# Two blocks on one core: high parts before low parts behind three norms, and the attention norm's scale inside its products

## What is computed

```
first block:
  h = rms_norm(x) * (1 + scale1) + shift1
  x = x + g1 * (hybrid mixer(h) @ w_o)
  h = rms_norm(x) * (1 + scale2) + shift2                 # norm N1 of the kernel
  x = x + g2 * ((silu(h @ w_fi[:, :F]) * (h @ w_fi[:, F:])) @ w_fo)
  x = rms_norm(x) * (1 + scale_f) + shift_f               # norm N2, the final modulate
second block:
  y = rms_norm(x, attn_norm)                              # norm N3
  q, k, v = split(y @ w_qkv);  x = x + attention(q, k, v) @ w_o2
  y = rms_norm(x, ffn_norm)                               # norm N4
  u = causal_conv(y @ w_up) + bias;  x = x + (silu(gate) * val) @ w_down
  out = rms_norm(x, final_norm)                           # norm N5
rms_norm(x, w) = x * rsqrt(mean(x * x) + eps) * w
```

## Time and profile before

| | |
|---|---|
| median of 3 runs | 975.1 us (972.58 to 975.62) |
| profiled execution, its own time | 974.01 us |
| its span in the profile | 972.2 us |
| PE busy | 926.5 us, 95% of the span, 7,996 matmuls |
| PE weight loads busy | 880.7 us, 91% |
| DVE busy | 667.2 us, 69% |
| ACT busy | 504.9 us, 52% |
| POOL busy | 65.2 us, 7% |
| mean granted clock of PE, as a share of full | 0.983 |

### The profile page before, as it was taken

One profiled execution on the slowest core, in us unless ns is written; L12 is line 12 of the kernel. 1 busy time (PEld: TensorE's weight loads), 2 busy tenths in 40 slices (PEclk: granted clock), 3 DMA queues, 4 the chain that ended last, 5 costly groups with the idle time before them and its releaser, 6 DMA issues.

```text
span 972.2 us, 18558 instructions
## 1 busy us (share of the span) xinstructions
PE 926.5 (95%) x7996; PEld 880.7 (91%) x7996; DVE 667.2 (69%) x1113; ACT 504.9 (52%) x821; POOL 65.2 (7%) x91
## 2 busy tenths in 40 slices
PE   5789999999999999999989999989999999999997
PEld 2588888898899999989989999979998999999997
DVE  3876677557579986778758875465656677777643
ACT  2476666544344556455334444465565566665442
POOL 0100012011000000030000001010000300000001
PEclk9799999999999999999999999999999999999999
DMA  8743222232249985446898775515343345555631
GB/s 321 265 157 127 88 88 91 85 131 88 88 158 359 351 299 219 174 179 253 253 290 318 265 241 186 197 43 197 131 140 108 107 177 196 186 174 166 235 120 44
DMA packets 27681, 177.31 MB, mean 182 GB/s; under 512 B 2864, under 2 KB 5680, under 8 KB 7504
## 3 DMA queue, kind: packets, MB, share of 16 engines
q1 hardware_dynamic: 27600, 176.13, 51.5%
HBM read 174.29 MB, written 1.84 MB: 181 GB/s over the span
## 4 chain that ended last, share of the span: by engine, by line
PE 71%; DVE 12%; ACT 7%; DMA 7%; issue 2%; SPq 0%; DVEq 0%; ACTq 0%
PE ps L1002 38%; PE ps L1008 19%; DVE wl L1696 3%; DMA raw<-in_w_fi_dram 3%; DVE acc L1631 2%; ACT wh L1343 2%; PE ps L1000 2%; DMA raw<-in_ada_dram 1%; DMA raw<-in_w_rest_dram 1%; DVE tmp L1658 1%; PE ps L1046 1%; DMA raw<-in_w_sc_dram 1%; PE ps L1140 1%; PE ps L1054 1%; PE ps L1201 1%
## 5 line engine op out<-in xcount | busy, mean ns | idle before, releaser
L1002 PE MATMUL ps<-HH,wh 128*128 128x256 f32 x1480 | 388.0, 294 | 6.4 <-DVE wl L1696 5.5
L1696 DVE TENSOR_TENSOR wl<-raw,wh 128x1024 fp32r<-128x1024 f32 x265 | 321.4, 1233 | 97.2 <-ACT wh L1343 96.5
L1002 PE MATMUL ps<-HH,wl 128*128 128x256 f32 x1480 | 375.2, 285 | 0.0
L1343 ACT ACTIVATE wh<-raw 128x1024 fp32r<-128x1024 f32 x265 | 272.6, 1040 | 171.8 <-PE ps L1008 105.3
L1002 PEld LDWEIGHTS ps<-HH,wh 128*128 128x128 f32 x1480 | 287.1, 194 | 15.8 <-issue 8.0
L1002 PEld LDWEIGHTS ps<-HH,wl 128*128 128x128 f32 x1480 | 287.1, 194 | 2.1 <-issue 2.1
L1008 PE MATMUL ps<-HL,wh 128*128 128x256 f32 x1480 | 241.5, 286 | 2.6 <-DVE HL L1671 2.2
L1008 PEld LDWEIGHTS ps<-HL,wh 128*128 128x128 f32 x1480 | 207.3, 194 | 3.3 <-DVE HL L1671 2.6
L1002 PE MATMUL ps<-FH,wl 128*128 128x256 f32 x352 | 88.8, 285 | 0.0
L1002 PE MATMUL ps<-FH,wh 128*128 128x256 f32 x352 | 88.1, 279 | 0.0
L1631 DVE SCALAR_TENSOR_TENSOR acc<-raw,silc,acc 128x512 f32<-128x512 f32 x101 | 76.6, 758 | 8.4 <-DMA raw<-in_ada_dram 5.2
(11 more groups left out here) (251 smaller groups left out, 1090.1 us busy)
## 6 DMA issues: line engine op xcount, KB each, us to landing
raw<-in_ada_dram SPq DMA_DIRECT2D x32, 1024.0 KB, 5.3
raw<-in_w_fi_dram SPq DMA_DIRECT2D x22, 1024.0 KB, 4.9
raw<-in_w_up_dram SPq DMA_DIRECT2D x22, 1024.0 KB, 4.8
raw<-in_w_rest_dram SPq DMA_DIRECT2D x20, 1024.0 KB, 4.8
raw<-in_w_in_dram SPq DMA_DIRECT2D x16, 1024.0 KB, 4.8
raw<-in_w_qkv_dram SPq DMA_DIRECT2D x12, 1024.0 KB, 4.8
raw<-in_w_o_dram SPq DMA_DIRECT2D x8, 1024.0 KB, 4.7
raw<-in_w_fo_dram SPq DMA_DIRECT2D x8, 1024.0 KB, 4.9
```

The lines of the kernel that those rows point to most:

```text
L1002: e.matmul(o, w[:, k, 128 * t:128 * t + 128], x_hi[:, k0 + k, :], start=first and n + k == 0, **MM)
L1343: e.activation(whl[u % HALF][0][:, 0:n], raw[i % RAW][:, c:c + n], ACT.Copy).then_inc(*a_hi.up(u))
L1696: e.tensor_tensor(wl[:, 0:n], raw[i % RAW][:, c:c + n], wh[:, 0:n].bitcast(F32), ALU.subtract).then_inc(*v_lo.up(u))
```

## The change

Five things:

1. Behind N1, N3 and N4 the low parts are no longer made between the scalings. `apply` writes all four `scale` and `high` events, then four `low` events; DVE makes all eight low parts, POOL none. The shift of N1 is one instruction per tile.
2. The two products behind each of these norms run through `high_first`: the 64 matmuls on the high activation of all four units, then the 32 on the low activation. The call of `split_up_to` in it goes no further than the fifth unit; the next units are put into the list only behind both products.
3. N2 and N3 share one R. `tmp = X * R` serves both: ACT makes `HH` from it with the weights `w1n` and `shn` (scale and shift times the attention norm's weight), DVE writes the block's output into X (`stream`) and the low part from X. The products `q2`, `k2`, `v2` then run on activations without N3's own scale.
4. N3's scale `R3` is made later: ACT squares the output, POOL adds the squares, and `third_scale` puts one summing matmul, Ln, Exp, and a copy times 0.125 (`R3q`) behind `k2` 0. `norm_col` turns R3 into a column for `v2`.
5. `q2` and `k2` are evacuated by DVE (`normed`, times R3q or R3) in place of ACT, `v2` by two ACT copies with the column as scale. The second sum of squares and its nine matmuls of no use are gone. `mod_scale` stands before `close`.

The function `in_turns` is added and called by nothing. The diff, cut:

```diff
-            if j:
-                parts(n, j - 1)
-        parts(n, 3)
+            emit("high", n, j, held[j])
+        for j in range(4):
+            if n == N3:
+                emit("stream", j, held[j])
+            emit("low", n, j, held[j])
+            tmp.give(held[j], v_norm, "lo", n, 2 * j + 1)
+            if n == N3:
+                s, before = sq.take()
+                emit("sq", N3, j, s, before, part[0] if j else None)
+                if j:
+                    sq.give(part[0], g_norm, "part", N3, j)
+                part[:] = [s]
...
+    def third_scale():
+        misc.order[:] = [b for b in misc.order if b[0] == 3]
+        bank, before = misc.take()
+        emit("norm_sum", N3, part[0], bank, before)
+        sq.give(part[0], p_norm, "sum", N3)
+        emit("norm_r", N3, bank)
+        made.add("norm_r3")
+        misc.give(bank, a_norm, "ln", N3)
+        yield
+        yield
+        bank, before = yield from take(misc)
+        emit("norm_col", N3, bank, before)
+        made.add("norm_col")
+        misc.give(bank, a_norm, "col")
+    def scaled_out(p):
+        kind, j, bank = p["kind"], p["j"], p["banks"][0]
+        while ("norm_col" if kind == "v2" else "norm_r3") not in made:
+            yield
+        if kind == "v2":
+            emit("plain", p["p"], 0)
+            main.give(bank, a_ev, "plain", p["p"])
+        else:
+            emit("normed", p["p"], 0)
+            main.give(bank, v_ev, "normed", p["p"])
+        made.add((kind, j))
+        if kind == "k2":
+            tasks.extend(attend(h) for h in range(4 * j, 4 * j + 4))
...
         elif kind in ("q2", "k2", "v2"):
-            emit("plain", p["p"], 0)
-            main.give(banks[0], a_ev, "plain", p["p"])
-            made.add((kind, j))
-            if kind == "k2":
-                tasks.extend(attend(h) for h in range(4 * j, 4 * j + 4))
+            begin(scaled_out(p))
...
-                bank, before = misc.take()
-                for i in range(4):
-                    emit("shift", n, i)
-                    if i:
-                        s, sfree = sq.take()
-                        emit("norm_sq", N3, i - 1, s, sfree, bank, before if i == 1 else None)
-                        sq.give(s, p_norm, "sq", N3, i - 1)
-                s, sfree = sq.take()
-                emit("norm_sq", N3, 3, s, sfree, bank, None)
-                sq.give(s, p_norm, "sq", N3, 3)
-                wbank, wfree = misc.take()
-                emit("norm_r", N3, bank, wbank, wfree)
-                misc.give(wbank, p_norm, "warm", N3)
-                misc.give(bank, a_norm, "ln", N3)
-                apply(N3)
-                misc.order[:] = [b for b in misc.order if b[0] == 3]
-            elif n == N4:
-                apply(n)
+            close(n, p)
+            for t in range(2):
+                main.give(banks[t], v_ev, "x", n, 6 + t)
+            if n == N5:
+                emit("finish")
             else:
-                emit("finish")
+                apply(N3 if n == N2 else n)
...
+    def open_banks(p):
+        count = 2 if p["split"] else 1
+        while len(main.order) < count:
+            assert tasks
+            tick()
+        taken = [main.take() for _ in range(count)]
+        p["banks"] = [b for b, _ in taken]
+        p["free"] = [f for _, f in taken]
+    def run_unit(p, n, last=None, part=None):
+        u = p["units"][n]
+        if part != "low":
+            split_up_to(u + HALF - 1 if last is None else last)
             low_of(u)
             if n == 0:
-                count = 2 if p["split"] else 1
-                while len(main.order) < count:
-                    assert tasks
-                    tick()
-                taken = [main.take() for _ in range(count)]
-                p["banks"] = [b for b, _ in taken]
-                p["free"] = [f for _, f in taken]
+                open_banks(p)
             until(*operands_of(p, units[u]))
-            tiles = p["width"] // 128
-            for t in range(tiles):
-                emit("mm", u, t)
-                if (n, t) != (len(p["units"]) - 1, tiles - 1):
-                    tick()
+        tiles = p["width"] // 128
+        for t in range(tiles):
+            emit("mm", u, t, part)
+            if part == "high" or (n, t) != (len(p["units"]) - 1, tiles - 1):
+                tick()
+    def close_product(p):
         after(p)
         tick()
...
+    def high_first(ps):
+        last = ps[0]["units"][0] + HALF - 1
+        for p in ps:
+            for n in range(2):
+                run_unit(p, n, last, "high")
+        for p in ps:
+            for n in range(2):
+                run_unit(p, n, last, "low")
+            close_product(p)
+    together = {("fg", 0): (high_first, ("fu", 0)), ("q2", 0): (high_first, ("k2", 0)),
+                ("ug", 0): (high_first, ("uv", 0))}
...
+        if key in together:
+            way, second = together[key]
+            way([p, named[second]])
+            if key == ("q2", 0):
+                begin(third_scale())
+        elif key not in [second for _, second in together.values()]:
+            for n in range(len(p["units"])):
+                run_unit(p, n)
+            close_product(p)
...
-    def pe_product(e, u, t):
+    def pe_product(e, u, t, part):
...
-        if first:
+        if first and part != "low":
             free(e, p["free"][b])
         v_lo.wait_ge(e, u)
-        for k in range(kn):
+        for k in range(kn) if part != "low" else ():
             high_of(e, src, k0 + k)
             for n, w in enumerate((wh, wl)):
...
-        for k in range(kn):
+        for k in range(kn) if part != "high" else ():
             low_part(e, src, k0 + k)
...
-        ins.then_inc(*p_mm.up(u, t))
+        if part != "high":
+            ins.then_inc(*p_mm.up(u, t))
...
-            a_ev.wait_ge(e, "plain", named["q2", j]["p"])
-            a_ev.wait_ge(e, "plain", named["k2", j]["p"])
+            v_ev.wait_ge(e, "normed", named["q2", j]["p"])
+            v_ev.wait_ge(e, "normed", named["k2", j]["p"])
...
+            elif kind == "norm_col":
+                b = ev[2]
+                free(e, ev[3])
+                a_norm.wait_ge(e, "r", N3)
+                for t in range(2):
+                    ins = e.matmul(psum[b][:, t:t + 1], R3[0:1, cs[t]], ones[0:1, 0:1], start=True, **MM)
+                ins.then_inc(*p_norm.up("col"))
+            elif kind == "norm_sum":
+                _, n, s, b, before = ev
+                free(e, before)
+                g_norm.wait_ge(e, "part", n, 3)
+                e.matmul(psum[b][:, 0:T], ones, sqs[s][:, 0:T], start=True, **MM).then_inc(*p_norm.up("sum", n))
...
+    def act_high(e, n, j, m):
+        finished(e, named[before_write[n]])
+        for kt in (2 * j, 2 * j + 1):
+            src, dst = tmps[m][:, T * (kt % 2):T * (kt % 2) + T], HH[:, kt, :]
+            v_norm.wait_ge(e, "scaled", n, kt)
+            if n == N1:
+                mod_ready(e, 6, 7)
+                ins = e.activation(dst, src, ACT.Identity, bias=modc[:, 24 + kt:25 + kt])
+            elif n == N3:
+                v_norm.wait_ge(e, "w1n")
+                ins = e.activation(dst, src, ACT.Identity, scale=w1n[:, kt:kt + 1], bias=shn[:, kt:kt + 1])
+            else:
+                ins = e.activation(dst, src, ACT.Copy)
+            ins.then_inc(*a_norm.up("hi", n, kt))
...
+        if n == N3 and j > 1:
+            x_ready(e, N2, 2 * j)
+            x_ready(e, N2, 2 * j + 1)
+            e.tensor_tensor(pair(tmps[m]), X[:, 2 * j:2 * j + 2, :], R[:, None, :].broadcast_to([128, 2, T]),
+                            ALU.mult).then_inc(*v_norm.up("scaled", n, 2 * j + 1))
+            v_norm.at[("scaled", n, 2 * j)] = v_norm.at[("scaled", n, 2 * j + 1)]
+            return
...
+    def dve_stream(e, j, m):
+        mod_ready(e, 12, 13)
+        v_norm.wait_ge(e, "w1c", N2, 0)
+        for kt in (2 * j, 2 * j + 1):
+            v_norm.wait_ge(e, "scaled", N3, kt)
+            e.tensor_scalar(X[:, kt, :], tmps[m][:, T * (kt % 2):T * (kt % 2) + T], w1c[:, kt:kt + 1],
+                            modc[:, 48 + kt:49 + kt], ALU.mult, ALU.add).then_inc(*v_norm.up("stream", kt))
+    def dve_low(e, n, j, m):
+        for kt in (2 * j, 2 * j + 1):
+            src, high = tmps[m][:, T * (kt % 2):T * (kt % 2) + T], HH[:, kt, :].bitcast(F32)
+            a_norm.wait_ge(e, "hi", n, kt)
+            if n == N1:
+                ins = e.scalar_tensor_tensor(out=HL[:, kt, :], in0=src, scalar=modc[:, 24 + kt:25 + kt], in1=high,
+                                             op0=ALU.add, op1=ALU.subtract)
+            elif n == N3:
+                v_norm.wait_ge(e, "stream", kt)
+                ins = e.scalar_tensor_tensor(out=HL[:, kt, :], in0=X[:, kt, :], scalar=v("attn_norm", kt), in1=high,
+                                             op0=ALU.mult, op1=ALU.subtract)
+            else:
+                ins = e.tensor_tensor(HL[:, kt, :], src, high, ALU.subtract)
...
```

(11 more changed lines are left out.)

137 lines of the change are left out of this document (63 added, 74 removed).

## The result

The changed kernel takes 982.23 us (median of four runs, 981.08 to 986.08), the kernel before 974.68 beside it: a ratio of 1.0103, with a 95% interval of 1.0071 to 1.0135. It is slower, by 1.0%. The profiled execution took 981.08 us, its span is 979.2; before it was 972.2.

What follows compares the result with a forecast made beforehand. PE was taken as the bound, busy 95% of the span, losing time only in waits or at half clock. Net losses of 2.1 + 2.4 + 4.1 = 8.6 us on 974.0 gave 982.6, forecast as 983 us, range 976 to 989.

Steps and rivals of the forecast that it cites:

- Entries: Losses at the norms shrink: N1 to 4.5 us, N2 with N3 to 4.5, N4 to 4.4; together 15.2 us gained.
- Behind N1, +2.1 us: Unit 101's subtraction queues behind an evacuation on DVE; PE waits 2.25 us, 0.65 later than before, plus 1.5 for clock.
- Unit 168: In k2 0's high phase PE waits 5.0 us for this subtraction, behind DVE's chain and five POOL additions at 0.5 each.
- The scores: Head 0's scores begin 7.8 us behind the end of N3's two products; PE waits 4.4 us.
- plus 1.5 for the clock: Behind the wait for head 0's scores, half clock costs PE another 1.5 us.
- 1.0 us, as most lie ahead of PE's need: In the attention, eight evacuations moved to DVE and waits for its division cost 0 to 4 us, taken as 1.0.
- the attention is bound by DVE: Rival: each head group waits on DVE's one queue, 1 to 1.5 us for each of four; 987 to 993 us, 13 in 100.
- Together at N3, +2.4 us: From N3 through the attention, the entry's 10.7 us gain is used up; net loss 2.4 us, including 1.4 and 1.0.
- Behind N4, +4.1 us: Unit 201's subtraction queues behind two convolutions; PE waits 5.6 us, begins 2.6 later than before, plus 1.5 for the clock.
- The sum: Over the whole kernel, net losses of 2.1, 2.4 and 4.1 us make 8.6 us.
- the subtractions come in time: Rival: DVE and ACT finish subtractions and rounding before they are needed, entries keep their gain; 959 us, half 970; together 7 in 100.
- 1.5 us for each short wait: Charge for half clock behind every new PE wait as long as the earlier ones of 1.87 and 3.01 us.

Runs made afterwards that it cites:

- low168_ahead: Changed kernel with unit 168's subtraction put ahead of R's first use on DVE; 977.2 us, ratio 1.0041.
- pool_narrow: Changed kernel with POOL's seven additions of squares for N3 cut to 2 of 256 columns each; 978.1 us, ratio 1.0053.
- fill_waits_2: Changed kernel with 8, 17, 16 and 24 matmuls of no use in PE's four new waits; 976.5 us, ratio 1.0041.
- q_behind_maxima: Changed kernel with DVE's evacuations of q2 1 to 3 one step later, behind the row maxima of the running heads; 979.1 us, ratio 1.0071.
- before_moved: Kernel before the change with one unused buffer of 64 bytes per partition behind w1c; 968.5 us, ratio 0.9943.
- lows_ahead_all: Changed kernel with unit 168's subtraction ahead of R's first use, later subtractions and roundings moved up at N1, N3 and N4; 962.6 us, ratio 0.9885.
- hh_moved: lows_ahead_all_q with 100 unused bytes ahead of HH and 28 behind HL; 955.7 us, ratio 0.9818.
- high_first_n3_only: Changed kernel with the products behind N1 and N4 in their former order, only N3's two high parts first; 977.2 us, ratio 1.0052.
- lows_ahead_all_q: lows_ahead_all with the evacuations of q2 1 to 3 behind the row maxima as well; 956.9 us, ratio 0.9848.

## Why the prediction was right

The forecast was 983 us, slower; 982.23 came. The mechanism was the one named: shorter entries, paid back by waits for work that stands behind later work in a list. But that the total is off by only 1 us is luck: two errors of some 4 us and of opposite sign lie in it, the attention and clock at N3 on one side and the places of buffers on the other.

- **Entries.** Right. N2 with N3: first matmul at 636.49, 4.08 us behind the first sum (4.05 forecast), loss 4.9 us against 4.5. N1 lost 4.7 against 4.5, N4 4.4 as forecast.
- **Behind N1, +2.1 us.** Right: a wait of 2.01 (2.25 forecast), 2.2 us late when unit 101 is done. Only 0.7 of that is left at N2, for a reason that the prediction had not: `fo` makes up 1.4 by its pace. The wait at 510, where a late kernel waits less, takes only 0.1.
- **Unit 168.** Right: a wait of 3.91 (5.0 forecast, 2.5 to 6), the price of a POOL addition 0.46 us (0.5 forecast). `low168_ahead` and `pool_narrow` show both causes, the queue and the lock.
- **The scores.** The wait is 3.84 against 4.4. The step "plus 1.5 for the clock" failed: behind the scores half clock lasted 6 us, not 3.5, and `fill_waits_2` puts it at some 2.7 us.
- **The attention, "1.0 us, as most lie ahead of PE's need".** This term was mis-sized: the changed kernel loses 3.3 us between the 169th product matmul of the stage and the end of the last `v2` product, and `q_behind_maxima` is 4.2 us ahead of it there. The prediction counted the evacuations' length, 0.6 us each. What counts is that those of `q2` 2 and `q2` 3 wait for PE, 4.51 us each, and hold the maxima behind them for that time. So the rival "the attention is bound by DVE" was right on this term, though not on the total.
- **Together at N3, +2.4 us.** Measured: 5.5, and 6.5 without the faster pace in `wo2`.
- **Behind N4, +4.1 us.** Right: a wait of 5.36 (5.6 forecast), 4.2 us late.
- **Left out.** The two new columns w1n and shn move the buffers behind them by 64 bytes, which by `before_moved` is worth 0.57% (0.38 to 0.75%), a gain of 4 to 7 us. The prediction looked at instructions alone. Beside `before_moved`, whose buffers lie in the same places but for those of the attention, the changed kernel is 1.6% slower, not 1.0%.
- **The sum.** Late by 2.2, 6.5 and 4.2 us makes 12.9, where 8.6 was forecast. The pace takes off 0.9 + 1.4 + 1.0 + 1.4 = 4.7, the wait at 510 takes 0.1 and the rest of the first stage 1.1: 7.0 us, the difference of the spans.

Of the rivals, "the subtractions come in time" describes `lows_ahead_all`: 959 us by the forecast, 962.6 measured. It needed two more edits than the change has.

## What to carry to other kernels

When a change lets an engine reach a point sooner, look in the lists of its suppliers for what it will ask for next: a supplier that stands idle for one input while a ready instruction is queued behind it costs a wait and then, more often than not, a stretch at half clock. Moving the subtractions and roundings up was worth 20 us here (982.2 to 962.6) and took some ten lines. And compare kernels whose buffers lie at the same places, or a shift in memory passes for a gain of the order.

## What had not been expected of the hardware

- **The pace of matmuls hangs on where their operand lies.** The same fp32r matmuls (128x256) start 0.1200 us apart with FH 36 bytes past a multiple of 128 and 0.1173 with FH 100 past it, counted from the first buffer. HH at 0 gives 0.120, at 100 0.1187. OHh gives 0.1201 at 36, 0.1185 at 100 and 0.1138 at 108. The remainder is not all: moved by another 128 bytes (`hh_moved`), FH gives 0.1178 and OHh 0.1200.
- **Half clock behind short waits, and not behind each.** The wait of 2.01 us behind N1 was followed by it in the changed kernel, `low168_ahead` and `q_behind_maxima`, and not in `pool_narrow`. One of 1.64 was not, in `pool_narrow`. The one of 1.87 between N2 and N3 was in the kernel before and was not in `before_moved`. One of 0.79 or 0.80 in the attention was in `lows_ahead_all`, `q_behind_maxima` and `high_first_n3_only`, and was not in the changed kernel or in `lows_ahead_all_q`. So 1.5 us for each short wait, as the prediction charged, is what it costs when it comes.
- **POOL holds DVE instructions of one tensor input too, and DVE holds POOL.** A pair of TENSOR_SCALAR of 256 columns took 1.58 us beside POOL's additions and 0.73 without. POOL's sixth addition, at 645.97 beside DVE's subtractions, took 2.83 us in place of 0.74.
